# Attention's PSUM banks in the order its transposed features free them, and the values' weights rounded at other places

## What is computed

```python
def swiglu(h, w_gu, w_down):
    g, u = jnp.split(h @ w_gu, 2, axis=-1)
    return (jax.nn.silu(g) * u) @ w_down

# the second block, after the gated mixer
x = x + swiglu(rms_norm_2(x, ffn_norm[0]), ffn_w_gu[0], ffn_w_down[0])
kv = rms_norm_2(x, kv_norm) @ kv_w              # keys, then values
q  = rms_norm_2(x, b_norm) @ b_w_q
a  = softmax(q0 k0 + bias) - lam * softmax(q1 k1 + bias)      # per head, causal
x  = x + (rms_norm_2(a @ v, subln) * (1 - lambda_init)).reshape(...) @ b_w_o
x  = x + swiglu(rms_norm_2(x, ffn_norm[1]), ffn_w_gu[1], ffn_w_down[1])
return rms_norm_2(x, final_norm)
```

## Time and profile before

| | |
|---|---|
| median of 3 runs | 1978.96 us (1975.62 to 1982.3) |
| the profiled execution | 1977.55 us, its span in the trace 1975.7 us |
| PE busy | 1912.0 us, 97% of the span |
| DVE, ACT, POOL busy | 1328.4, 1024.6, 204.6 us (67%, 52%, 10%) |
| chain that ended last | PE 84%, DVE 8%, the rest 8% |
| layer 0's products end, attention's first matmul | 1359.7 us, 1371.4 us |
| attention, layer 1 | 1371 to 1618 us, 1619 to the end |

### The profile page before, as it was taken

How to read it: one execution, slowest core, us unless ns; L and a number is a source line. 1 busy time by engine, 2 the same in 40 slices (tenths; PEclk the granted TensorE clock), 3 DMA queues, 4 the chain that set the end, 5 groups by cost and what they waited for, 6 DMA issues and landing times.

```text
span 1975.7 us, 23073 instructions
## 1 busy us (share of the span) xinstructions
PE 1912.0 (97%) x8818; PEld 1536.0 (78%) x8818; DVE 1328.4 (67%) x1698; ACT 1024.6 (52%) x1562; POOL 204.6 (10%) x273
## 2 busy tenths in 40 slices
PE   5999999999999999999999999998999999999997
PEld 4668768888888888768788888886777778888886
DVE  6667699999999999773543835648344452745737
ACT  4443278888888888744232423326455542332423
POOL 3100211031201110020010000001020110000001
PEclk9999999999999999999999999999999999999999
DMA  8565579999999999951232061313221133051211
GB/s 298 163 214 188 181 274 363 375 376 377 369 374 362 373 363 366 342 186 64 86 128 86 7 207 43 132 60 95 79 64 65 43 117 130 20 192 64 85 64 43
DMA packets 200027, 366.51 MB, mean 186 GB/s; under 512 B 13514, under 2 KB 84055, under 8 KB 199914
## 3 DMA queue, kind: packets, MB, share of 16 engines
q1 hardware_dynamic: 181152, 343.20, 49.4%
q10 hardware_dynamic: 8714, 11.17, 1.7%
q0 software_dynamic: 10048, 10.62, 1.6%
HBM read 365.05 MB, written 24.65 MB: 197 GB/s over the span
## 4 chain that ended last, share of the span: by engine, by line
PE 84%; DVE 8%; DMA 2%; issue 2%; ACT 2%; POOL 1%; ACTq 0%; POOLq 0%; DVEq 0%
PE ps L351 81%; DVE wlo L297 3%; DMA raw<-in_w_expert_gate 2%; PE ps L2312 1%; DMA VR<-in_b_subln 1%; PE ps L2339 1%; DVE X L2926 1%; ACT whi L277 1%; PE ps L3137 0%; ACT YB L2404 0%; PE ps L887 0%; POOL small L855 0%; DVE ATl L2917 0%; DVE AT5l L2917 0%; DVE XT0l L2395 0%
## 5 line engine op out<-in xcount | busy, mean ns | idle before, releaser
L297 DVE TENSOR_TENSOR wlo<-raw,whi 128x1024 fp32r<-128x1024 f32 (+1 forms) x598 | 697.4, 1210 | 227.4 <-ACT whi L277 224.2
L277 ACT ACTIVATE whi<-raw 128x1024 fp32r<-128x1024 f32 (+1 forms) x598 | 594.2, 1046 | 278.3 <-PE ps L351 248.2
L351 PE MATMUL ps<-hT3h,whi 128*128 128x512 f32 x352 | 137.0, 389 | 0.6 <-DVE hT3l L348 0.6
L351 PE MATMUL ps<-hT5h,whi 128*128 128x512 f32 x352 | 137.0, 389 | 0.6 <-DVE hT5l L348 0.6
L351 PE MATMUL ps<-hT3h,wlo 128*128 128x512 f32 x352 | 136.9, 389 | 0.0
L351 PE MATMUL ps<-hT5h,wlo 128*128 128x512 f32 x352 | 136.9, 389 | 0.0
L351 PE MATMUL ps<-hT3l,whi 128*128 128x512 f32 x352 | 136.9, 389 | 0.0
L351 PE MATMUL ps<-hT5l,whi 128*128 128x512 f32 x352 | 136.9, 389 | 0.0
L2949 DVE TENSOR_TENSOR XN<-XN,ps 128x512 f32<-128x512 f32 x44 | 30.1, 688 | 129.1 <-PE ps L351 128.4
L2881 ACT ACTIVATE XN<-ps 128x512 f32<-128x512 f32 x44 | 26.3, 597 | 165.2 <-PE ps L351 163.4
L351 PE MATMUL ps<-whi,XT1h 128*128 128x512 f32 x256 | 102.7, 401 | 1.5 <-DVE XT1l L2395 1.5
(11 more groups left out here) (491 smaller groups left out, 4165.3 us busy)
## 6 DMA issues: line engine op xcount, KB each, us to landing
raw<-in_w_expert_gate SPq DMA_DIRECT2D x64, 1024.0 KB, 7.4
raw<-in_w_expert_up SPq DMA_DIRECT2D x64, 1024.0 KB, 8.4
raw<-in_w_expert_down SPq DMA_DIRECT2D x64, 1024.0 KB, 7.1
raw<-in_ffn_w_gu SPq DMA_DIRECT2D x44, 1024.0 KB
raw<-in_ffn_w_down SPq DMA_DIRECT2D x16, 1024.0 KB, 8.0
raw<-in_ada_w SPq DMA_DIRECT2D x24, 512.0 KB, 5.0
raw<-in_a_w_in SPq DMA_DIRECT2D x8, 1024.0 KB, 9.7
raw<-in_kv_w SPq DMA_DIRECT2D x8, 1024.0 KB, 4.9
```

What stands on the lines that cost most here:

```text
L277: e.activation(hi[:, c], x, ACT.Copy).then_inc(self.S("w_hi"), 1)
L297: e.tensor_tensor(lo[:, c], halves[h], hi[:, c].bitcast(F32), ALU.subtract).then_inc(self.S("w_lo"), 1)
L351: return e.matmul(o, l, r, start=start, stop=stop, skip_group_check=True)
```

## The change

Four edits. Attention's division of the banks is no longer a list of numbers: it takes the banks of `tf3` in the order of its eight groups. Those are 0, 1, 4, 5, 6, 7, 2, 3, so `rest` becomes (0, 1), `keys` (4, 5), `turned` (6, 7, 2) and `sums` (3). In `ffn_vec` the adds of product 2 stand straight behind those of product 7, then half the remainder of `vv` item 0 (only in layer 0; `low_half` is new), then product 4's first add, before `then(0)`; the other half of the remainder goes behind the last normalization. In `attn_act` the rounding of `vv` item 1 moves from the middle of `rows_act` to behind the eight copies of the features. `low` can now stop in the middle of a weight.

```diff
--- before.py
+++ after.py
@@ -122,7 +122,7 @@
         self.S, self.items, self.w, self.ends, self.index = S, [], [], {}, {}
         self.raw, self.hi, self.lo = [], [], []
         self.done_by, self.after, self.since, self.quads, self.held, self.sum = [], [], {}, [], {}, []
-        self.mids = 0
+        self.mids = self.halved = 0
         self.raw_places, self.raw_last, self.raw_count, self.raw_of = [0, 1], {}, {}, []
         self.raw_more = None
         self.places, self.place_last, self.place_of, self.gain = [0, 1], {}, [], []
@@ -284,17 +284,26 @@
                         m.then_inc(self.S("w_hi"), 1)
             self.n_hi += 1
 
-    def low(self, e, upto):
+    def low_half(self, e):
+
+        self.low(e, self.n_lo + 1, 1)
+
+    def low(self, e, upto, halves=2):
 
         while self.n_lo < min(upto, len(self.w)):
             j, (i, a, b) = self.n_lo, self.w[self.n_lo]
             n = a * b
             z = self.place_of[j][0]
-            hi, lo, gain, halves = self.hi[z], self.lo[z], self.gain[j], self.halves(j)
+            hi, lo, gain, raws = self.hi[z], self.lo[z], self.gain[j], self.halves(j)
             for h, c in enumerate((slice(0, n // 2), slice(n // 2, n))):
+                if h < self.halved:
+                    continue
+                if h == halves:
+                    self.halved = 1
+                    return
                 e.wait_ge(self.S("w_hi"), 2 * j + h + 1)
                 if gain is None:
-                    e.tensor_tensor(lo[:, c], halves[h], hi[:, c].bitcast(F32), ALU.subtract).then_inc(self.S("w_lo"), 1)
+                    e.tensor_tensor(lo[:, c], raws[h], hi[:, c].bitcast(F32), ALU.subtract).then_inc(self.S("w_lo"), 1)
                 else:
                     raw = self.raw[self.raw_of[i][0]]
                     for k in range(h * a // 2, (h + 1) * a // 2):
@@ -302,6 +311,7 @@
                         m = e.scalar_tensor_tensor(out=lo[:, c], in0=raw[:, c], scalar=gain(k), in1=hi[:, c].bitcast(F32),
                                                    op0=ALU.mult, op1=ALU.subtract)
                     m.then_inc(self.S("w_lo"), 1)
+            self.halved = 0
             self.n_lo += 1
 
     def parts(self, j):
@@ -753,7 +763,8 @@
         ffn_plan(0)
         R.plan("tf3", 8, V_)
 
-        rest, keys, turned, sums = (collections.deque(z) for z in ((2, 3), (1, 4), (5, 6, 7), (0,)))
+        freed = [R.groups["tf3", kc][4] for kc in range(KC)]
+        rest, keys, turned, sums = (collections.deque(z) for z in (freed[0:2], freed[2:4], freed[4:7], freed[7:8]))
 
         def qk_plan(*heads):
             for h in heads:
@@ -2983,15 +2994,17 @@
                 else:
                     add(f0, 7, 0)
                     add(f0, 7, 1)
-                    W.low(e, js[6] + 2)
                     add(f0, 2, 0)
                     add(f0, 2, 1)
+                    if js[6] + 1 < len(W.w):
+                        W.low_half(e)
+                    add(f0, 4, 0)
                     then(0)
-                    add(f0, 4, 0)
                     add(f0, 4, 1)
                     then(1)
                     then(2)
                     then(3)
+                    W.low(e, js[6] + 2)
 
 
         LAM = tmpT[0][:, 0:256].rearrange("p (a d) -> p a d", a=4)
@@ -3336,9 +3349,10 @@
             def take(name, i):
                 W.high(e, W.index[name][i] + 1)
 
-            rows_act(e, 0, lambda i: take("vv", 1) if i == 3 else None)
+            rows_act(e, 0, lambda i: None)
             e.dma_start(tmpT[0][:, 0:256], g["b_lambda_2"][0].rearrange("a d -> (a d)").partition_broadcast(P)).then_inc(S("lam"), 16)
             features_act(e, 3, hT4, None)
+            take("vv", 1)
             e.wait_ge(S("lam_sum"), 1)
             e.activation(ls[:, 2:4], ls[:, 0:2], ACT.Exp).then_inc(S("lam_exp"), 1)
             take("k", 0)
```

## The result

The changed kernel takes 1975.26 us (median of 18 runs, 1970.67 to 1984.57), the kernel before, run beside it, 1980.84 us (18 runs, 1975.0 to 1988.77). The ratio is 0.9971, with a 95% interval from 0.9957 to 0.9985: 5.7 us less, of which the interval leaves 3.0 to 8.5.

The account below looks back on a forecast made before the run. PE, at 97% of the span, was taken to bound the kernel, except at the seam, where it waits for seven hT4l. 4.85 + 1.42 - 0.35 = 5.92 us off 1978.96 gives 1973.0 us, range 1969.5 to 1977.5.

Parts of the forecast that it names:

- The bank: Seam of layer 0 and attention: with bank 0 the first values' group waits for feature group 0 alone; no other cost.
- the bank is not the gate: Rival at the seam: PE starts with the seventh hT4l for another reason; near 1978.1 us, chance 0.04.
- When the features come: Seam, chain of square, root and normalization: row 3's normalization starts at 1363.65, 1.83 us sooner than 1365.48.
- The hold: POOL at the seam stands still during DVE's SBUF-only instructions; row 0's line 853 ends at 1357.73, its power near 1358.40.
- term 1: Seam: PE starts the values at 1366.50 behind the first hT4l instead of 1371.35; 4.85 us gained.
- the last normalization comes no sooner: Rival at the seam: POOL is held more often than counted; 3.0 us gained there, 1974.9 us, chance 0.10.
- The clock: Values' first matmuls at the seam: with the long pause gone, PE keeps full clock; 1.42 us by the tenth matmul.
- Term 2: Values' first ten matmuls at full clock take 2.14 us instead of 3.56; 1.42 us gained, bounds 0 and 1.42.
- the row I leaned on: Profile row 1586.3 to 1587.8: PE stood 1.5 us and kept clock 1.00; taken as grounds for the full 1.42 us.
- The second weight: Item 1's rounding and remainder behind the features, ready near 1373.4; PE asks at 1377.4, hidden by 4 us; costs nothing.
- Term 3: Program's end, layer 1: last(0) later, row 2's power ends at 1966.7; 0.35 us lost, bounds 1.0 lost and 1.0 gained.
- the end gets shorter: Rival at the program's end: row 2's root gets between DVE's multiplications; 1 us gained, 1971.7 us, chance 0.09.

Follow-up runs that it names:

- the remainder whole: Changed kernel with all four remainder instructions of the values' first weight behind the last normalization; 1975.01 us in one run.
- the filled gap: Kernel before with three idle matmuls on PE between the seam's transposes and the values, results never read; 1977.59 us in one run.
- old adds: Changed kernel with layer 1's adds in the old order, product 4's first add behind last(0); layer 0 keeps the new order; 1976.28 us in one run.
- stores behind the squares: Changed kernel with ACT's waits and store issues for finished rows moved behind all its squares at the program's end; 1979.45 us in one run.
- both at the end: Changed kernel with layer 1's adds in the old order and ACT's stores behind its squares; 1972.31 us in one run.
- the last kernel: Changed kernel with the remainder's first half behind row 2's normalization and ACT's stores behind its squares; median 1974.65 us, ratio 0.9970 to before.

## Why the prediction was right

The forecast was 5.92 us less; the trace shows 5.92 from Z to the end, and the timed runs 5.7. That the two agree to the last digit is luck: small misses cancelled, so the terms count. The forecast time, 1973.0 us, is 2.3 us under the measured 1975.26, and 1.9 of that is the level it started from: before took 1978.96 us in three runs and 1980.84 in 18. The gain of 0.29% lies just under the 0.3% at which the forecast had put the line between faster and same, though the interval leaves out no change.

- **The bank** was the gate. With the banks alone PE starts behind the first `hT4l`, 3.45 us sooner. The rival "the bank is not the gate" is refuted by that run.
- **When the features come.** Forecast: row 3's normalization 1.83 us sooner; measured 2.11. The hold was placed right and sized wrong: I had POOL's line 853 stretched to over 1 us and the power at its usual length, with row 0's root ready at Z - 0.89. POOL got in between the two remainder instructions, each of its two was held by one of them (0.55 and 0.96 us), and the root ended at Z - 1.22. For row 2 I expected line 850 to get in ahead of row 1's normalization. It did (0.22 us), and line 864 (853 in before) behind it (0.19 us); then the power was held (1.05 us). Row 0 itself gained little by its earlier root: its normalization stands behind product 4's add and starts at Z - 1.01, with the remainder whole too. The half remainder cost 0.58 us (from row 3's normalization to `hT4l` it is 2.12 us, before 1.54), forecast 0.60. From `hT4l` to PE it is 0.83 us where I had 0.71. So 0.28 more, 0.02 more and 0.12 less: **term 1 measures 5.03 instead of 4.85**. The rival "the last normalization comes no sooner" is refuted.
- **The clock.** **Term 2 measures 1.39 instead of 1.42**, and the kernel with the filled gap gives the cause by itself. The Trainium skill (TensorE: Matmul & The Clock Gate, "A second HAM failure mode: psum-queue depth-cycling") has the clock swing under frequent tiny pauses; by it the bursts would have run low too. No trace here shows them so: the bursts, with pauses of up to 1.2 us between them, kept 1.00 in all 14, and so did the values behind them in eight of the nine in which PE started within 9 us of Z. But the margin was smaller than I thought: 0.99 us before the values did no harm in any of seven traces, 2.32 us did with the remainder whole. And the row I leaned on, 1.5 us of standing at full clock at the end of attention, does not bear what I put on it: PE stands there for the same 1.56 us in all 14 traces, and in seven of them, after among them, the clock falls between 0.4 us before its return and 1.0 us behind it. Term 2 came out whole; that reason for it was not good. Whether the falls there are of the kind that the Trainium skill describes is open.
- **The second weight** cost nothing. ACT's rounding ran 1380.93 to 1383.55 and DVE's remainder 1383.10 to 1385.83; PE asks near 1390, 4 us behind, and has no pause there.
- **Term 3 measures 0.26 lost instead of 0.35**, by the very chain forecast: old adds take it back. The rival "the end gets shorter" came true only with the stores behind the squares: 355.98, 0.80 us less than before.
- **Not in the sum**: the fall of the clock at the end of attention, 0.2 us in after's own trace (6.18 to layer 1's first matmul against 5.03 + 1.39 = 6.42). The two kernels in which it stayed away, stores behind squares and both at the end, are 6.41 and 6.49 us ahead of before there. Just behind it, at 1591.86, before waited 1.00 us for DVE in any case, which may hide part of it. With it the terms give 5.03 + 1.39 - 0.26 - 0.24 = 5.92.
- **The parts don't add.** I costed bank and clock as separate terms. The banks alone give 4.40 us, the rest alone 0.43, together 4.83 and not 5.92. PE's starts do add: 3.45 and 1.53 us against 5.03. It is the clock that doesn't: the banks alone win 1.40 us of it at the tenth matmul, the rest alone loses 0.44 there, and more behind it, because its low stretch is 6.8 us long instead of 3.4. At the 192nd of the values' matmuls the gains are 4.88, 0.70 and 6.46 us, so 0.9 us belong to neither part. To the end it is 1.1; the rest falls together with the low clock at the end of attention, which the traces of the banks alone and of after have and the other two have not. The forecast's sum had these 0.9 us only because both edits are made together.

## What to carry to other kernels

Where a new group of matmuls starts late, look at which bank it takes and who frees that bank last; handing banks on in the order they come free was worth three quarters of this change in the traces. A pause that long costs twice, once as a wait and once in the clock behind it, so two edits that shorten the same pause must be tried together as well as apart. And compare traces from a common point behind the scatter (here Z), since 12.9 us of scatter ahead of layer 0 would have hidden the whole effect.

## What was not expected of the hardware

- The clock can fall after PE is back at work: at full clock up to 1369.0 with PE restarted at 1368.33, then 0.51, after a pause of only 2.32 us. In before it was already low when PE came back from 3.91 us.
- The low stretch lasted 3.4 us in before and with ACT's rounding alone, behind a pause of 3.91 us, and 6.8 us in the two traces in which the pause was 4.48 us (all but the banks, DVE's order alone). That the longer pause made it longer is not shown apart.
- Of the 14 traces, all with PE's stand of 1.56 us at the end of attention, seven show the low clock there (after, its repeat, the old adds, the last kernel, the banks alone, DVE's order alone, before with the gap filled) and seven don't.
- POOL gets in between two DVE instructions that follow each other without a gap: 0.55 us for one that takes 0.19 alone, ending between the two remainders, and 0.96 us for the next.
